# The scores of a unit stand between the two dense chunks of their step, in block 2's mixers

## What is computed

```python
def hybrid_mixer(x, positions, w_in, conv_w, rel_bias, w_out):
    proj = jnp.einsum('bsd,dp->bsp', x, w_in)
    (cb, cc, ch, dq, dk, dv, iq, ik, iw, cq, ck, cv) = jnp.split(proj, offs, axis=-1)
    y_conv = short_conv_mixer(cb, cc, ch, conv_w)
    ...
    y_dsa = dsa_attention(dq, dk, dv, iq, ik, iw)       # top 128 keys of a query, by an index score
    y_chk = chunk_band_attention(cq, ck, cv, rel_bias)  # all keys of earlier chunks, with a bias
    y = jnp.concatenate([y_conv, y_dsa, y_chk], axis=-1)
    return jnp.einsum('bsm,md->bsd', y, w_out)
```

## Time and profile before

| | |
|---|---|
| median of 3 runs | 2872.36 us (2870.85 to 2875.64) |
| the profiled execution's own time | 2872.17 us |
| its span | 2870.3 us |
| PE busy | 2783.8 us, 97% of the span |
| DVE busy | 1645.2 us, 57% |
| ACT busy | 1247.1 us, 43% |
| POOL busy | 420.6 us, 15% |
| granted TensorE clock, mean | 0.995 |

### The profile page before, as it was taken

The page is one execution under the profiler, slowest core; times in us unless marked ns, Lnnn a source line. Parts: engine busy times, 40 slices in busy tenths (PEclk is TensorE's granted clock), DMA queues, the critical chain, the costliest instruction groups (busy, mean ns, idle before and its releaser), DMA issues.

```text
span 2870.3 us, 39078 instructions
## 1 busy us (share of the span) xinstructions
PE 2783.8 (97%) x15782; PEld 2355.4 (82%) x15782; DVE 1645.2 (57%) x2469; ACT 1247.1 (43%) x2085; POOL 420.6 (15%) x337
## 2 busy tenths in 40 slices
PE   8999999999989999999999999999999999999997
PEld 7878999999877788887668888888776688888886
DVE  5786545454777745454876466333658764663335
ACT  5574322234675422223554545333445545453333
POOL 2222000001222000001343120000313431200003
PEclk9999999999999999999999999999999999999999
DMA  4112222232112333332123223333221232233232
GB/s 144 52 45 67 89 89 85 93 95 82 52 45 68 95 98 95 98 94 93 56 74 118 88 74 96 96 96 96 85 81 56 75 124 87 68 99 100 92 100 66
DMA packets 71922, 244.35 MB, mean 85 GB/s; under 512 B 9152, under 2 KB 10816, under 8 KB 71744
## 3 DMA queue, kind: packets, MB, share of 16 engines
q1 hardware_dynamic: 66528, 235.50, 25.8%
q10 hardware_dynamic: 5216, 6.36, 0.7%
HBM read 239.73 MB, written 2.10 MB: 84 GB/s over the span
## 4 chain that ended last, share of the span: by engine, by line
PE 87%; DVE 8%; ACT 3%; issue 1%; POOL 1%; DMA 0%; ACTq 0%; DVEq 0%
PE psum L578 24%; PE psum L584 24%; PE psum L581 24%; PE psum L650 2%; PE psum L673 1%; PE psum L677 1%; PE psum L675 1%; DVE temp L2186 1%; PE psum L1077 1%; DVE small L2184 1%; PE psum L1089 1%; PE psum L911 1%; DVE weights_hi_lo L1749 1%; PE psum L964 1%; PE psum L939 1%
## 5 line engine op out<-in xcount | busy, mean ns | idle before, releaser
L578 PE MATMUL psum<-act_hi_lo,weights_hi_lo 128*128 128x264 f32 (+2 forms) x2544 | 777.9, 345 | 3.8 <-ACT temp L1287 2.8
L581 PE MATMUL psum<-act_hi_lo,weights_hi_lo 128*128 128x264 f32 (+2 forms) x2544 | 752.6, 335 | 1.9 <-DVE weights_hi_lo L1749 1.9
L584 PE MATMUL psum<-act_hi_lo,weights_hi_lo 128*128 128x264 f32 (+2 forms) x2544 | 752.3, 335 | 0.0
L1749 DVE TENSOR_TENSOR weights_hi_lo<-weights_float,weights_hi_lo 128x1024 fp32r<-128x1024 f32 (+2 forms) x446 | 556.8, 1249 | 223.4 <-ACT weights_hi_lo L1178 222.0
L1178 ACT ACTIVATE weights_hi_lo<-weights_float 128x1024 fp32r<-128x1024 f32 (+2 forms) x446 | 463.7, 1042 | 502.6 <-PE psum L584 431.8
L578 PE MATMUL psum<-hidden_hi_lo,weights_hi_lo 128*128 128x512 f32 (+2 forms) x1584 | 519.7, 358 | 3.8 <-DVE x_residual L2002 1.5
L584 PE MATMUL psum<-hidden_hi_lo,weights_hi_lo 128*128 128x512 f32 (+2 forms) x1584 | 511.6, 353 | 2.2 <-POOL hidden_hi_lo L2012 2.2
L581 PE MATMUL psum<-hidden_hi_lo,weights_hi_lo 128*128 128x512 f32 (+2 forms) x1584 | 511.0, 352 | 0.0
L578 PEld LDWEIGHTS psum<-act_hi_lo,weights_hi_lo 128*128 128x128 f32 x2544 | 440.0, 189 | 68.4 <-issue 17.8
L581 PEld LDWEIGHTS psum<-act_hi_lo,weights_hi_lo 128*128 128x128 f32 x2544 | 439.3, 189 | 47.9 <-issue 2.6
L584 PEld LDWEIGHTS psum<-act_hi_lo,weights_hi_lo 128*128 128x128 f32 x2544 | 438.8, 189 | 48.0
(11 more groups left out here) (283 smaller groups left out, 3290.2 us busy)
## 6 DMA issues: line engine op xcount, KB each, us to landing
weights_float<-in_w_ff SPq DMA_DIRECT2D x128, 512.0 KB, 3.6
weights_float<-in_w_gu SPq DMA_DIRECT2D x88, 512.0 KB, 3.6
weights_float<-in_w_in SPq DMA_DIRECT2D x70, 512.0 KB, 3.7
weights_float<-in_w_down SPq DMA_DIRECT2D x32, 448.0 KB, 3.3
weights_float<-in_w_out SPq DMA_DIRECT2D x16, 512.0 KB, 3.6
weights_float<-in_w_down SPq DMA_DIRECT2D x16, 512.0 KB, 3.5
weights_float<-in_w_mv SPq DMA_DIRECT2D x16, 512.0 KB, 3.2
weights_float<-in_w_mix SPq DMA_DIRECT2D x16, 512.0 KB, 3.3
```

The costliest lines, as they stand in the source:

```text
L578: e.matmul(slot[:, place:place + c1 - c0], w_hi[:, col], x_hi[:, c0:c1], start=first, stop=False)
L581: e.matmul(slot[:, place:place + c1 - c0], w_lo[:, col], x_hi[:, c0:c1], start=False, stop=False)
L584: mm = e.matmul(slot[:, place:place + c1 - c0], w_hi[:, col], x_lo[:, c0:c1], start=False, stop=final)
L1749: e.tensor_tensor(lo[:, 0:cols], K.staged(n)[:, 0:cols], hi[:, 0:cols].bitcast(F32), ALU.subtract).then_inc(*K.did("lo", n))
```

## The change

The call of `step(s)`, which gives out the scores of the unit that begins at this step, moves from the head of the loop's body to a place between the step's two `dense` calls: `k` is 2q and then 2q + 1, and the call stands in front of the odd one.

```diff
     for s in range(TOK_STEPS, MEM_STEP):
-        step(s)
         t, quarter = divmod(s - TOK_STEPS, 4)
         kind, n = ORDER2[t]
         if quarter == 0:
             B.clear(t % 2)
         for k in (2 * quarter, 2 * quarter + 1):
+            if k % 2:
+                step(s)
             dense(e, w, K, PIECE["w_in2", l, SLOT2[kind, n]], K.bank[t % 2], k, K.act_chunk(k, T2),
                   (K.hi_there("in2", l, k), K.lo_there("in2", l, k)), k == 0, k == DC - 1, T2,
                   mark=("half_read", l) if s == MEM_STEP - 3 and k == DC // 2 - 1 else None)
```

## The result

| | before | after |
|---|---|---|
| median | 2872.66 us (2869.87 to 2876.04) | 2877.78 us (2874.53 to 2880.46) |
| ratio | | 1.0016, 95% interval 1.0010 to 1.0022 |
| the profiled execution's own time | 2872.17 us | 2880.46 us |
| its span | 2870.3 us | 2878.6 us |
| mean granted clock | 0.995 | 0.993 |

The change costs 5.1 us at the median, 0.16 to 0.18% of the kernel. That is inside the 0.2% that the prediction calls no change, though the interval shows that it is a loss. The forecast was 2877.5. All medians and ratios here leave out two executions of e5_light_head (3095 and 3451 us, at a granted clock of 0.85 and 0.75), the only ones in a slower state.

The account below looks back on a forecast made before the run. PE, busy for 97% of the span, was taken as the bound. Per layer, 4.62 of borders less 1.5, 0.42 and 0.42, plus 0.08 and 0.27, gave 2.63; both layers +5.3, so 2877.5 us, range 2872.4 to 2882.4.

Parts of the forecast that it names:

- Step (a): On PE, each moved unit cuts its dense run, adding a head and tail (a border): 0.21 us, 4.6 a layer.
- Rival B: Mid-step borders cost nothing, the scores' weight load running under the previous product; only returned waits count: 2869.4 us, chance 0.08.
- Step (b): Before scores of units 7, 15 and 21, the later start covers PE's waits: 1.5 us a layer returned.
- The mask: Before unit 21's scores, PE's wait for the selection mask would be returned by the later start: 0.57 us.
- the tie: At unit 21's scores, the delayed mask and PE itself would both arrive at 1479.9, the sum's thinnest point.
- Absorbed before transposes: Borders of units 12 and 14 vanish in PE's waits for `part_lo`, which DVE sets: 0.42 us a layer.
- The gaps at units 1, 10 and 11: Short PE gaps of 0.05 to 0.2 us cover part of the borders: 0.42 us a layer.
- Step (c): Later scores make DVE slip where its cover is thin: 0.50 us at unit 8, up to 1.4 at unit 20.
- Unit 18's transposes: They wait longer for POOL: the reciprocal slips 0.85 us, PE arrives 0.58 later, costing +0.27.
- Units 8 and 9 together: DVE's slip of 0.50 us sets the path and contains two borders (0.42), costing 0.08 more than them.
- Rival A: DVE's lag at units 4 to 9 and 16 to 21 is not covered, cancelling returns: 9.1 us slower, chance 0.25.
- Rival C: The DVE-bound part swallows borders; only the eight of units 0 to 7 are paid: +2.1 us, chance 0.15.

Follow-up runs that it names:

- e5_light_head: The kernel before, with each top-k search keeping 2 of its 16 steps so that DVE is not full: 2868.63 us, 0.9981.
- e9_mask_first: The changed kernel, with the selection mask's products ahead of the scores in the top-k units: 2878.33 us, 1.0019 against the kernel before.
- e4_three: The kernel before, with only the scores of units 7, 15 and 21 moved between the dense calls: 2872.46 us, 0.9996.
- e1_tail: The kernel before, with the scores of the 44 units moved behind both dense chunks of their step: 2881.79 us, 1.0032.
- e6: The changed kernel, with each top-k search keeping 2 of its 16 steps: 2875.92 us, 1.0009 against the kernel before.
- e7: The kernel before, with unit 8's reciprocal one step earlier in DVE's queue: 2871.91 us, 0.9995.
- e8: The kernel before, with units 7, 15 and 21 moved and the reciprocals of units 8 and 18 one step earlier: 2871.24 us, 0.9995.
- e10: The kernel before, with units 7, 11, 15 and 21 moved and unit 8's reciprocal one step earlier: 2868.45 us, 0.9985.
- e3_d_only: The kernel before, with only the 10 top-k units with steps under 92 in each layer moved: 2873.29 us, 1.0002.

## Why the prediction was right

**Step (a), a border costs 0.21.** Held: 0.204 as the mean of the eleven plain ones (0.16 to 0.24), in the middle of steps that the trace of before could not show. That is 0.13 us a layer less than priced. Rival B fell on the same rows: the weight load of L911 starts with its product, at 1403.90. The Trainium skill, page "TensorE: Matmul & The Clock Gate", section "Architectural detail: the array is 16× 32×32, not 1× 128×128", says that PE's queue can pull weight loads ahead of products. The trace agrees for the dense loads (L584's at 1477.61 in e9_mask_first, its product at 1477.83) and not for the 64-row loads of the scores, which start with their product (1403.90 and 1403.90 after).

**Step (b), waits returned.** Predicted 1.5 a layer before scores; the ledger gives 0.48 + 0.46 + 0.47 = 1.41. The mask was put at 0.57, and that is the term mis-sized: unit 21's scores now start 0.36 behind the last product (1484.17 to 1484.53), 0.03 over a plain tail, so the tie went narrowly to the mask. In e4_three, where DVE does not slip, unit 21 returns 0.32 and not 0.27, so the tie is about half of the 0.10; the rest stays open. Absorbed before transposes: 0.42 predicted, 0.41 measured. The rows of the tie, after:

```profile
1484.17 0.39 PE L584 MATMUL psum<-act_hi_lo,weights_hi_lo 128*128 128x512 f32 x1
1484.53 1.13 PE L911 MATMUL psum<-arena 64*128 64x512 f32 x4
```

The gaps at units 1, 10 and 11 were put at 0.42 and are 0.14 + 0.23 + 0.02 = 0.39. That sum is in part luck: each was put between 0.05 and 0.2, and two of the three lie outside.

**Step (c), what the later start costs.** DVE's slip went as priced: against unit 15 its maxima come 0.30 later at unit 16 (0.3 predicted) and 1.35 at unit 20 (1.4). Unit 18's transposes: +0.27 predicted, +0.29 measured. But the prediction misread which wait that is. The 0.3 us that it finds in the earlier trace rows stand at 1496.79, beside `w_mv` and behind the stretch; unit 18's second half starts at 1469.70, 0.64 behind its first, and after 0.92 behind it (1474.27 to 1475.19). Before, then after:

```profile
1469.70 0.31 PEld L928 LDWEIGHTS psum<-consts,temp 128*128 128x128 f32 x3 [0.38 <-POOL temp L2542]
...
1496.79 0.66 PE L928 MATMUL psum<-consts,temp 128*128 128x128 f32 x4 [0.30 <-POOL temp L2542]
```

```profile
1475.19 0.55 PE L928 MATMUL psum<-consts,temp 128*128 128x128 f32 x3 [0.43 <-POOL temp L2543]
```

The term did not hang on the 0.3 (it is DVE's slip less PE's delay), so its size is unharmed. PE's listed waits for POOL rose from 2.0 to 2.5 us for this reason and not by a quarter: 0.4 at unit 18, which was under the list's threshold, and 0.1 more at unit 8. Those for `part_lo` shrank by 0.1, as predicted. Units 8 and 9 together: 0.08 more than their borders was predicted, and it was 0.06 less. DVE did slip: the bias of unit 8 moved from 1400.67 to 1405.10, which is 1.55 later against the start of the stretch, 0.49 more than PE's offset of 1.06 as it came there. The prediction put this at 0.50. But the reciprocal slipped by 1.41 only (1407.47 to 1411.76): before, the product of the rotation (L2163) came 1.29 behind the maximum, after 1.14, and this 0.15 of slack in DVE's own queue I had not looked for. The growth of DVE's waits for scores was put at 6 to 9 us and is 5.7, just under.

**The sum.** 22 x 0.204 = 4.49, less 1.41, 0.41, 0.39 and 0.06, plus 0.29: 2.51, with rounding the 2.49 of layer 0, and 2.41 in layer 1, against 2.63. The error is borders (0.13) and the pair 8 and 9 (0.14) on the one side, the mask (0.1) on the other. For both layers that is 4.9 for 5.3. The forecast was right by its mechanism and only a little helped by errors that cancel.

**Rival A** (9.1 us) fell: DVE's slip came before PE's at unit 18, as priced, and by 0.03 us at the mask, and nowhere else did it take a return away. How near it was e1_tail shows. **Rival C** (2.1 us) fell by the ledger: in the saturated part, units 15 to 21, borders of 0.16 to 0.24 are paid one by one, and with DVE's load taken off (e5, e6) the move costs only 0.9 us a layer more. That the time outside the stretches would stay as it was is shown only by the medians (5.1 against 4.9); the single pair of profiles has 3.4 us of its own there.

## What to carry to other kernels

On an engine that is nearly without idle time, as PE here, a change between kinds of instruction can have a price (0.2 us in this case): read it from one place in the trace where the new layout already stands, multiply, and subtract only waits that you can name, each against what will be late next. A blanket move pays the border everywhere and earns only where something waited; move just those few. Expect a wait that is removed to return in part at the next resource in the queue (e7, e8), and look whether the engine that is early now lies over another's work; moving the next consumer too kept most of it (e10). Where a single execution scatters as much as the effect, cut both traces at unmoved instructions and compare the stretch.

## What the runs showed of the hardware that I had not expected

**The clock can fall behind two short stalls, and not always.** In 18 of the 24 layers profiled, PE waited 0.84 to 1.61 us before the first half of unit 8's transposes and 0.82 or 0.83 before the second. In three of these 18 (e3_d_only layer 0, e1_tail layer 1, e6_light_middle layer 1) the granted clock fell for a few microseconds from its level of 2.4 GHz to that of 1.2. PE of e3_d_only behind the transposes that had waited 0.82, and then its window of 4 us (length; busy of PE, PEld, DVE, ACT, POOL; clock; DMA):

```profile
1410.06 0.77 PE L578 MATMUL psum<-act_hi_lo,weights_hi_lo 128*128 128x512 f32 x1
1410.63 0.63 PE L581 MATMUL psum<-act_hi_lo,weights_hi_lo 128*128 128x512 f32 x1
1411.06 0.63 PE L584 MATMUL psum<-act_hi_lo,weights_hi_lo 128*128 128x512 f32 x1
```

```profile
1410.00:1414.00 4.00, 4.00 (x14) 2.65 (x15) 0.25 (x3) 1.66 (x2) 3.69 (x3) 0.63 0.41 133
```

Products stand 0.43 apart instead of 0.23, and the layer is 1.4 to 1.6 us longer. Code with the same stalls kept the full clock in the other fifteen, before's and after's among them. What makes the difference stays open. In e7, e8 and e10, where one stall of 0.28 to 0.30 is left, no such fall was seen in six layers. That is too few to say that the early reciprocal prevents it.

**The same POOL instruction takes 1.3 or 2.2 us, and the longer ones lie under DVE's weight split.** The rotation's product of 128x512 (L2550, L2549 before) runs seven times a layer, 168 times in the twelve traces. 162 of them took 1.26 to 1.32 us, and DVE's weight split (L1749 before, 128x1024) lay over them by 0.08 us at most. The six others took 2.16 to 2.19, and lay under that split for 1.03 to 1.05: they are one product a layer in e7, e8 and e10, the runs with unit 8's reciprocal early. The slowing does not come from the start being later: in e7 the product starts where it did before. DVE's search steps (L2184, L2186) lay over products of 1.27 us for 1.0 us without harm. No run moves the split alone, so that it is the cause is argued from this, not shown by a run of its own.
